# Six expert-weight buffers instead of four in a mixture-of-experts loop, with the final norm row loaded late

## The reference, cut to what matters

```
def _moe(x, router_w, router_bias, w_gate, w_up, w_down, sh_gate, sh_up, sh_down):
    ...
    _, idx = lax.top_k(scores + router_bias.astype(jnp.float32), TOP_K)        # 8 of 64 experts per token
    ...
    hid = jax.nn.silu(jnp.einsum('td,edf->tef', t, w_gate)) * jnp.einsum('td,edf->tef', t, w_up)
    routed = jnp.einsum('tef,efd->td', hid * gates[..., None], w_down)
    shared = (jax.nn.silu(t @ sh_gate) * (t @ sh_up)) @ sh_down
    ...
x = x + gate2 * _moe(...)
y = _rmsnorm(x, final_g)
```

## Time and profile before

| | us |
|---|---|
| median of 3 runs (lowest, highest) | 1445.11 (1444.06, 1445.9) |
| the profiled execution, its own time | 1442.61 |
| its span, first to last instruction | 1440.8 |
| PE busy in the span | 1269.3 (88%) |
| DVE, ACT, POOL busy | 672.2, 436.9, 384.3 |
| first weight DMA of the expert loop issued | 890.26 |
| first and last static `gate_up` start | 932.08 and 1346.18 |
| first read of `y_rows` issued | 1374.92 |

### The profile page before, as it was taken

How to read it: one execution, slowest core, us unless ns; L and a number is a source line. 1 busy time by engine, 2 the same in 40 slices (tenths; PEclk the granted TensorE clock), 3 DMA queues, 4 the chain that set the end, 5 groups by cost and what they waited for, 6 DMA issues and landing times. The chain is left out here.

```text
span 1440.8 us, 19850 instructions
## 1 busy us (share of the span) xinstructions
PE 1269.3 (88%) x7564; PEld 912.9 (63%) x7564; DVE 672.2 (47%) x1217; ACT 436.9 (30%) x827; POOL 384.3 (27%) x471
## 2 busy tenths in 40 slices
PE   5999999999899998999799998688897878797965
PEld 1678666777899986555545456566565757576721
DVE  2698738202655664677676225554121211121147
ACT  3212221215566555233141014122222222232331
POOL 0200100102311211454440110345453544454200
PEclk9999999999999999999999999899998999899989
DMA  9656666121101001000120302568897979898688
GB/s 360 211 174 186 207 41 59 59 72 30 38 16 37 23 16 34 6 7 10 57 99 21 142 0 85 209 214 326 297 372 285 382 287 362 306 364 310 242 328 334
DMA packets 100853, 238.14 MB, mean 165 GB/s; under 512 B 28836, under 2 KB 47014, under 8 KB 99352
## 3 DMA queue, kind: packets, MB, share of 16 engines
q1 hardware_dynamic: 82088, 194.89, 41.0%
q0 software_dynamic: 18672, 42.00, 7.9%
HBM read 220.63 MB, written 37.14 MB: 179 GB/s over the span
## 5 line engine op out<-in xcount | busy, mean ns | idle before, releaser
L2870 PEld LDWEIGHTS PS<-arena 128*128 128x128 f32 x1536 | 186.4, 201 | 61.3 <-DMA arena<-in_exp_w_down 46.4
L2870 PE MATMUL PS<-arena 128*128 128x128 f32 x1536 | 191.5, 286 | 33.8 <-DMA arena<-in_exp_w_down 27.2
L3247 DVE TENSOR_TENSOR arena<-arena,PS 128x128 f32<-128x128 f32 x48 | 13.8, 289 | 258.1 <-ACT arena L3456 198.8
L3567 POOL DMA_INDIRECT arena<-h_rows,arena x116 | 117.6, 1013 | 36.1 <-issue 35.1
L2893 PE MATMUL PS<-arena 128*128 128x512 f32 (+1 forms) x288 | 113.8, 598 | 1.0 <-DVE arena L3247 0.9
L3577 POOL DMA_INDIRECT y_rows<-arena x60 | 60.5, 1008 | 195.0 <-ACT arena L3462 172.2
L915 PE MATMUL PS<-arena 128*128 128x320 f32 x384 | 107.9, 434 | 1.5 <-DVE arena L1337 1.5
L920 PE MATMUL PS<-arena 128*128 128x320 f32 x384 | 107.3, 432 | 0.0
L3456 ACT ACTIVATE arena<-PS 128x128 f32<-128x128 f32 x60 | 16.6, 277 | 256.9 <-PE PS L2870 114.8
L915 PEld LDWEIGHTS PS<-arena 128*128 128x128 f32 x384 | 72.1, 190 | 32.7 <-issue 2.3
L920 PEld LDWEIGHTS PS<-arena 128*128 128x128 f32 x384 | 73.0, 190 | 30.4
(11 more groups left out here) (518 smaller groups left out, 2198.0 us busy)
## 6 DMA issues: line engine op xcount, KB each, us to landing
arena<-in_exp_w_gate SPq DMA_DIRECT2D x64, 512.0 KB
arena<-in_exp_w_up SPq DMA_DIRECT2D x64, 512.0 KB
arena<-in_exp_w_down SPq DMA_DIRECT2D x64, 512.0 KB
arena<-y_rows SPq DMA_DIRECT2D x40, 512.0 KB, 15.0
arena<-in_w_in SPq DMA_DIRECT2D x16, 1024.0 KB, 6.2
arena<-in_w_mod SPq DMA_DIRECT2D x32, 512.0 KB, 3.6
arena<-in_w_mod SPq DMA_DIRECT2D x4, 1024.0 KB, 14.2
arena<-in_w_mod SPq DMA_DIRECT2D x2, 2048.0 KB, 13.7
```

The costliest lines, as they stand in the source:

```text
L2870: mm = pe.matmul(PS[:, p, col:col + P], w[:, k, :], xT[p][:, k, :], start=k == 0, stop=k == KT - 1)
L3567: pool.indirect_dma_start(xg[j][:, g, :], None, T["h2_rows"], bass.IndirectOffsetOnAxis(rows[:, g:g + 1], 0), bounds_check=4 * TOK - 1, oo ...
```

## The change

There are six weight slots (`W`) instead of four; `U` stays 4 for the token and result buffers. Each slot now has two places: gate and up (2048 words) and down (1024 words). Slot 0 stays. Slot 1 takes the place of `gate_row[:, 0]` and of `fin_row`. Slot 2 is the old slot 1 (and holds the shared expert's weights), slots 3 and 4 are the old 2 and 3. Slot 5 lies over `acc[:, 0]` to `acc[:, 2]`. Load n waits for the last user of load n-6. SP reads six expert numbers before the first load, issues loads 0 and 1 at once, load 2 after `s_ps`, loads 3 and 4 after `h2_out`, and load 5 after a new wait, for all five calls of `own`. From load 6 on it reads number n+1 before it waits for slot n. `fin_row` gets the old place of slot 0's down weights and is loaded after the tail's weights. ACT waits for the last static block instead of `f_own` before it writes `acc` in the combination.

```diff
-        fin_row = part(r1_at + 14336, 1024)
+        fin_row = part(r2_at + 13312, 1024)
...
-        ew = [part(a, 3072) for a in (r2_at + 11264, r2_at + 14336, r1_at + 8192, r1_at + 11264)]
-        eg = [w[:, 0:1024].rearrange("p (k f) -> p k f", k=KT) for w in ew]
-        eu = [w[:, 1024:2048].rearrange("p (k f) -> p k f", k=KT) for w in ew]
-        ed = [w[:, 2048:3072] for w in ew]
+        ew_at = [(r2_at + 11264, r2_at + 13312), (r2_at, r1_at + 14336), (r2_at + 14336, r2_at + 16384),
+                 (r1_at + 8192, r1_at + 10240), (r1_at + 11264, r1_at + 13312), (r2_at + 6144, r2_at + 8192)]
+        W = len(ew_at)
+        egu = [part(a, 2048) for a, _ in ew_at]
+        eg = [w[:, 0:1024].rearrange("p (k f) -> p k f", k=KT) for w in egu]
+        eu = [w[:, 1024:2048].rearrange("p (k f) -> p k f", k=KT) for w in egu]
+        ed = [part(b, 1024) for _, b in ew_at]
...
-                sp.dma_start(fin_row, T["final_g"].rearrange("(a n) -> a n", a=1).to_broadcast([P, D])).then_inc(o_fg, 16)
...
-                def load_rank(n):
-                    e = sp.value_load(block_expert[0:1, loads[n]:loads[n] + 1], min_val=0, max_val=NE - 1)
-                    if n >= U:
-                        sp.wait_ge(e_ps, last_use[n - U] + 1)
-                    load_block(e, n % U)
+                def expert_of(n):
+                    return sp.value_load(block_expert[0:1, loads[n]:loads[n] + 1], min_val=0, max_val=NE - 1)
 
                 sp.wait_ge(m_order, 1)
-                load_rank(0)
+                ranked = [expert_of(n) for n in range(W)]
+                load_block(ranked[0], 0)
+                load_block(ranked[1], 1)
                 for t in range(NT):
                     sp.wait_ge(b_cp, 2 * t + 2)
                     sp.dma_start(h2_tokens[t * P:(t + 1) * P], h2[:, t, :]).then_inc(h2_out, 16)
 
                 sp.wait_ge(s_ps, 2 * NT)
-                load_rank(1)
+                load_block(ranked[2], 2)
                 sp.wait_ge(h2_out, 16 * NT)
-                for n in range(2, NE - 2):
-                    load_rank(n)
+                load_block(ranked[3], 3)
+                load_block(ranked[4], 4)
+                sp.wait_ge(f_own, NT)
+                load_block(ranked[5], 5)
+                e = expert_of(W)
+                for n in range(W, NE - 2):
+                    now = e
+                    if n + 1 < NE - 2:
+                        e = expert_of(n + 1)
+                    sp.wait_ge(e_ps, last_use[n - W] + 1)
+                    load_block(now, n % W)
...
-                        load_block(e, LIST + j)
-
+                        load_block(e, LIST_W + j)
+
+                sp.wait_ge(e_ps, last_use[60] + 1)
+                sp.dma_start(fin_row, T["final_g"].rearrange("(a n) -> a n", a=1).to_broadcast([P, D])).then_inc(o_fg, 16)
...
-                    act.wait_ge(f_own, NT)
+                    if t < 3:
+                        act.wait_ge(e_ps, STATIC)
```

More of the change, by code:

```diff
@@ L2343, in trunk_program @@
         MAGIC = 12582912.0
-        ew = [part(a, 3072) for a in (r2_at + 11264, r2_at + 14336, r1_at + 8192, r1_at + 11264)]
-        eg = [w[:, 0:1024].rearrange("p (k f) -> p k f", k=KT) for w in ew]
-        eu = [w[:, 1024:2048].rearrange("p (k f) -> p k f", k=KT) for w in ew]
-        ed = [w[:, 2048:3072] for w in ew]
+        ew_at = [(r2_at + 11264, r2_at + 13312), (r2_at, r1_at + 14336), (r2_at + 14336, r2_at + 16384),
[5 more added lines that the diff above has]
+        ed = [part(b, 1024) for _, b in ew_at]
+        SHW, OWN_W = 2, 5
         sact, sup, shid = (part(a, TOK) for a in (r2_at + 4096, r2_at + 4736, r2_at + 5376))
@@ L2415, in trunk_program @@
         e_mid, e_mT = sem("e_mid"), sem("e_mT")
-        e_w, e_x = [sem(f"e_w{j}") for j in range(U)], [sem(f"e_x{j}") for j in range(U)]
+        e_w, e_x = [sem(f"e_w{j}") for j in range(W)], [sem(f"e_x{j}") for j in range(U)]
         e_turn, e_tr, e_xT, e_gu, e_silu, e_hid, e_ps, e_y = (sem("e_" + n) for n in "turn tr xT gu silu hid ps y".split())
@@ L2449, in trunk_program @@
         halves = [sum(len(blocks[c][1]) > 1 for c in range(b + 1)) for b in range(STATIC)]
-        LIST = STATIC % U
-        assert len(loads) % U == LIST == 2 and [last_use[NE - 2 - U + j] for j in range(2)] == [STATIC - U + j for j in range(2)]
+        LIST, LIST_W = STATIC % U, len(loads) % W
+        assert 60 % W == 0 and LIST == LIST_W == 2 and max(last_use[NE - 2 - W + j] - j for j in range(2)) <= STATIC - U
         def by_vector(b):
@@ L2495, in _ @@
                 wd = T["exp_w_down"].rearrange("a e f d -> f (a e) d")
-                sp.dma_start(eg[1], T["sh_w_gate"].rearrange("a (p k) f -> p (a k) f", k=KT)).then_inc(s_w, 16)
-                sp.dma_start(eu[1], T["sh_w_up"].rearrange("a (p k) f -> p (a k) f", k=KT)).then_inc(s_w, 16)
-                sp.dma_start(ed[1], T["sh_w_down"].rearrange("a f d -> f (a d)")).then_inc(s_w, 16)
+                sp.dma_start(eg[SHW], T["sh_w_gate"].rearrange("a (p k) f -> p (a k) f", k=KT)).then_inc(s_w, 16)
+                sp.dma_start(eu[SHW], T["sh_w_up"].rearrange("a (p k) f -> p (a k) f", k=KT)).then_inc(s_w, 16)
+                sp.dma_start(ed[SHW], T["sh_w_down"].rearrange("a f d -> f (a d)")).then_inc(s_w, 16)
                 sp.dma_start(index, T["index"]).then_inc(m_idx, 16)
@@ L2761, in _ @@
                 pe.wait_ge(s_w, 48)
-                shared_in(eg[1], 0, 0)
+                shared_in(eg[SHW], 0, 0)
                 pe.wait_ge(o_rw, 16)
@@ L2809, in shared_down @@
                         pe.wait_ge(s_acc, n - 3)
-                    pe.matmul(PS[:, n % 4, :], shid[:, t * P:(t + 1) * P], ed[1][:, 512 * half:512 * half + 512],
+                    pe.matmul(PS[:, n % 4, :], shid[:, t * P:(t + 1) * P], ed[SHW][:, 512 * half:512 * half + 512],
                               start=True, stop=True).then_inc(s_ps, 1)
@@ L2823, in rows_by_expert @@
                     pe.matmul(PS[0:1, 6, 5 * NE:6 * NE], rank_col, ident[:, 0:NE], start=True, stop=True).then_inc(m_rrow, 1)
-                shared_in(eg[1], 0, 1)
+                shared_in(eg[SHW], 0, 1)
                 count()
@@ L2829, in _ @@
                 ranks()
-                shared_in(eu[1], 2, 0)
+                shared_in(eu[SHW], 2, 0)
                 rows_by_expert()
@@ L2833, in _ @@
                 row_transpose(3)
-                shared_in(eu[1], 2, 1)
+                shared_in(eu[SHW], 2, 1)
                 for n in range(4, 2 * NT):
@@ L2876, in gate_up_halves @@
                             r = slice(HD * n, HD * n + HD)
-                            both = ew[j][:, 0:2 * D].rearrange("p (w k f) -> p k w f", w=2, k=KT)[:, k]
+                            both = egu[j].rearrange("p (w k f) -> p k w f", w=2, k=KT)[:, k]
                             mm = pe.matmul(PS[r, p, 0:2 * P].rearrange("p (w f) -> p w f", w=2), xT[p][:, k, n:P:2], both,
@@ L2901, in _ @@
                     for n in used:
-                        pe.wait_ge(e_w[n % U], 48 * (n // U + 1))
+                        pe.wait_ge(e_w[n % W], 48 * (n // W + 1))
                     x_ready(b)
                     if len(used) > 1:
-                        gate_up_halves(b % 2, [n % U for n in used])
+                        gate_up_halves(b % 2, [n % W for n in used])
                     else:
-                        gate_up(b % 2, used[0] % U)
+                        gate_up(b % 2, used[0] % W)
                     if b + 1 < STATIC and by_vector(b + 1) is None:
@@ L2910, in _ @@
                     if b:
-                        down(b - 1, (b - 1) % 2, [n % U for n in blocks[b - 1][1]], b <= 2)
+                        down(b - 1, (b - 1) % 2, [n % W for n in blocks[b - 1][1]], b <= 2)
                     if len(used) > 1:
                         turn_halves(b)
-                down(STATIC - 1, (STATIC - 1) % 2, [n % U for n in blocks[-1][1]])
+                down(STATIC - 1, (STATIC - 1) % 2, [n % W for n in blocks[-1][1]])
                 groups = group_count(pe)
@@ L2920, in _ @@
                         if j:
-                            down(2 * i + STATIC, 0, [LIST])
-                        pe.wait_ge(e_w[LIST + j], 48 * i + 48 * (len(loads) // U + 1))
+                            down(2 * i + STATIC, 0, [LIST_W])
+                        pe.wait_ge(e_w[LIST_W + j], 48 * i + 48 * (len(loads) // W + 1))
                         pe.wait_ge(e_xT, 2 * i + (COPIES + j + 1))
-                        gate_up(j, LIST + j)
-                    down(2 * i + (STATIC + 1), 1, [LIST + 1])
+                        gate_up(j, LIST_W + j)
+                    down(2 * i + (STATIC + 1), 1, [LIST_W + 1])
                 for t in range(NT):
```

## The result

The changed kernel takes 1400.15 us (median of 4 runs, 1397.99 to 1401.7), the kernel before 1444.59 us (median of 4). The ratio is 0.9702, with a 95% interval of 0.9665 to 0.9738: 44 us less, where 35 us were forecast; 1400 lies in the range and just under the forecast's own 1402 to 1417. The profiled execution took 1397.99 us, its span is 1396.2 us, 44.6 us less than before. Of these, 46.0 us were gained in the loop (block 0 to block 57: 1346.18 - 932.08 = 414.1 us before, 1301.89 - 933.80 = 368.1 us after); block 0 started 1.7 us later.

The account below looks back on a forecast made before the run. The prediction took the DMA engines and a four-slot ring that at times starves them to bound the loop in turn. Block 57 starting 35 us earlier, other edits zero, took 1445 to 1410 us, range 1397 to 1428.

Parts of the forecast that it names:

- the forecast's own 1402 to 1417: Whole kernel: the most likely band for the measured time in us, given a chance of 0.55.
- The cause: Expert loop: four slots at times leave the DMA engines without work; the idle tenth, 39 us, is recoverable with more slots.
- The other edits at zero: Reading ahead, six early reads, load 1 earlier and late `fin_row` gain or cost nothing; the six reads take 3.8 us, covered.
- The start: Loop start: fifth `own` ends at 965.0, load 5 issues at 965.1, block 5 starts about 974, 6 us later than before.
- The sum: Loop's DMA work from 965.1: last static weights at 1306 plus 5 us, block 57 about 1311, 35 us earlier.
- The busy-time figure, 1313: Loop: arrival in us of the last static weights if the remaining 348 us of DMA busy time run from 965.1.
- What bounds the loop: After the change the DMA engines bound the loop, PE waiting a little before most blocks with some 25 us to spare.
- PE's floor: Loop from block 5 at 974: PE's own work takes 311 us, ending block 57 at 1285.
- The rate of 362 GB/s for a whole loop: Rival: slower DMA engines start block 57 at 1321, gain 25, total 1420 us; its band 1417 to 1430 had 0.20.
- The Trainium skill's rule on the HBM side: Rival: HBM limits loop loads to some 358 GB/s, gain 21, total 1424 us; chance 0.07, inside a 0.20.
- Late scatters: Rival in the loop: scatters stretched beyond near 19 us of slack slow each block, 1472 us at 27 us latency; slower 0.03.
- The byte-rate rival: Rival: loop bytes move at 381 GB/s with nothing lost, block 57 at 1299, gain 47, total 1398; band 1390 to 1402, 0.14.

Follow-up runs that it names:

- four_new: The changed kernel with four weight slots instead of six, every other part of the change kept; 1443.83 us, ratio 1.000 against the kernel before.
- six_twothirds: The changed kernel (six slots) without the down weights of loads 6 to 61, two thirds of the bytes per expert; 1388.36 us, ratio 0.9614.

## Why the prediction was right, point by point

**The cause** was right: four slots left the DMA engines idle in a loop that they bound. With the depth undone (four_new) the gain is gone, and with the depth the share is 0.99. The other edits at zero: shown for reading ahead by itself, and for the rest as a group by four_new. The six reads moved the issue of load 0 from 890.26 to 894.86, 4.6 us where 3.8 were reckoned. In the chain it was the tokens' transfer, which ended at 930.46, and not weights, that released block 0.

**The start** was right to within 0.3 us for the end of `own` and the issue of load 5, and to 0.5 us for block 5. A part of this is luck: block 0 started 1.7 us later than before, which the forecast did not have, and a wait of 1.45 us that PE had before block 1 was gone, so that block 4 again came at 958.10. The new wait's price has been measured: 9.5 us in the medians, 6 us in the profiled loops. The prediction saw the 6 us at block 5 but did not ask for the simple way round it. The engines were not quite idle until 965: from 950 on they had a share of 0.48 at 153 GB/s.

**The sum** was mis-sized by 9 us, at the term for the last static weights: "I take the middle, 1306, and add 5 us". The byte rate of 381 GB/s was right (measured 380 over 328 us). The busy-time figure, 1313, was wrong: 348 us of busy time were reckoned with, and 0.99 x 328 = 325 us were used. Per MB that is 2.61 us where it was 2.74 before (352 us for 128.6 MB). That busy time counts half-filled stretches as full would explain this; no run tests it. Taken by bytes alone the weights would arrive at 1299; the last transfer was issued at 1280.2 and took 16.7 us, so it landed at 1296.9. The 5 us for the slowest transfer were put on top of bytes; the traffic itself thinned out near 1293 (share 0.65 in 1290 to 1293, 0.30 in 1293 to 1297), so an allowance of 4 us for the last landing was real, and the bytes were 2.5 MB too many (127.1 against 0.380 x 328 = 124.6). About as much, 0.153 x 15 = 2.3 MB, had moved from 950 to 965, ahead of the point from which the sum starts.

**What bounds the loop** was half right. I expected the DMA engines to hold PE "a little before most blocks", with 25 us to spare on PE. In fact PE ran without a gap for up to 18 blocks together (5 to 22) and waited only at block 5 and before the halves blocks 23, 32 and 41, which take two experts at once. "Never 8 us before a halves block" held for these three (6.45 at most), not for block 5, which is in halves too and waited 11.00. Block 57 started at 1301.9, some 5 us behind the landing of its weights, as PE's own sequence had it. PE's floor, 311 us to the end of block 57 or 305 to its start, was right (306.7 measured without weights, in one execution). Floor and DMA work lay closer together than the sum made them: block 57 could have started at 974.5 + 306.7 = 1281.2, its weights landed at 1296.9, and it started at 1301.9, the three waits and their slow restarts behind the floor.

**The rivals.** The rate of 362 GB/s for a whole loop did not occur. The Trainium skill's rule on the HBM side (DMA: Bandwidth & Descriptors, Where 436 GB/s comes from, some 358 GB/s per core) would, by the prediction's estimate, have given 1424 us; this case's trace does not agree, the loop ran at 380 GB/s for 328 us and at 401 for 60. Late scatters: the last one still took 2.9 us, the 52 from 965 to 1300 had a median of 7.6 and a maximum of 9.3 us from issue to landing, under the 19 us of slack, and PE waited for none. The byte-rate rival, 1398, came nearest, but only its rate was right by itself: PE's own sequence ended the loop 3 us behind it.

**What stays open:** the spread of the run without weights, and ACT's waits with an unnamed releaser (8 of them, 44.1 us, in the kernel before, 20 with 109.0 us in six_twothirds), which every profile has but that of the changed kernel. What PE waited for `middle` in `turn_halves` was 4.9 us in six_twothirds and at most 2.2 us in any other. Nor does a run say why the DMA share still dips behind blocks 32 and 41.

## What to carry to other kernels

These rules are drawn from this one loop. When a ring of buffers refills from the consumer's progress, count what is still outstanding at the moment the consumer waits: if it is less than one period's work, the transfer engines idle, and one more buffer may bring nearly all there is (here 45 us for the fifth). A buffer that becomes free late should not be the next in turn, for all that stands behind it in SP's queue is late too: the sixth was worth nothing as next in turn (1400.15 us against 1398.45 with five) and 8 us with a later turn. Size the work left by bytes over the rate of the saturated windows, which came within 3 us here where busy time was 16 us off, and don't expect much of another buffer when the share is 0.99.

## What the runs showed of the hardware that was not expected

Weights, gathers and scatters mixed moved 387 GB/s over 85 us (975 to 1060) and 401 over 60 us (1230 to 1290) in the changed kernel; the saturated windows of before lay between 362 and 405. In the changed kernel, too, 10 us at a share of 1.02 (1100 to 1110) moved only 357 GB/s, so a share of 1 does not fix the rate, and whether the deeper queue raised it is not shown. A single expert's 1.57 MB, with gathers and scatters beside it but no other weights, took 8 us from SP's first issue (965.42) to the start of its block (973.40), not much less than the 9.7 us with four more experts queued behind it; in the full queue of the changed kernel the last transfer of an expert took 14.8 us (median) from issue to landing.
